# Second expert table: token-major products instead of feature-major, and no closing transposes

## The reference, cut to what matters

```python
def chunk(args):
    x_c, e_c, g_c = args
    u = u_tab[e_c]
    vv = v_tab[e_c]
    a = jax.nn.gelu(jnp.einsum('cd,chkd->chk', x_c, u).astype(jnp.float32), approximate=False)
    return jnp.einsum('chk,chkd->cd', (g_c * a).astype(vv.dtype), vv)
...
x = x + gate2[:, None, :] * peer_ffn(h2, ...)
return rmsnorm(x, norm_final_g)
```

## Time and profile before

| | |
|---|---|
| median of 3 runs | 1925.5 us (1924.06 to 1925.86) |
| span of the profiled execution | 1923.2 us |
| what lies around the span, by these runs | 0.9 to 2.7 us, 2.3 at the median |
| TensorE busy / VectorE busy / ScalarE busy | 91% / 67% / 47% |
| bytes from memory, mean rate | 280 MB, 147 GB/s |
| half A / half B | 1478 to 1719 us / 1721 to 1906 us |

### The profile page before, as it was taken

One profiled execution on the slowest core, in us unless ns is written; L12 is line 12 of the kernel. 1 busy time (PEld: TensorE's weight loads), 2 busy tenths in 40 slices (PEclk: granted clock), 3 DMA queues, 4 the chain that ended last, 5 costly groups with the idle time before them and its releaser, 6 DMA issues.

```text
span 1923.2 us, 32571 instructions
## 1 busy us (share of the span) xinstructions
PE 1748.6 (91%) x11846; PEld 1612.2 (84%) x11846; DVE 1286.6 (67%) x2392; ACT 906.5 (47%) x1411; POOL 23.9 (1%) x50
## 2 busy tenths in 40 slices
PE   6788898898978886997979999999999999999996
PEld 5677777796767675886779999899999999999996
DVE  3666557544755686444656999777777888875554
ACT  4474355344534573443335666555554333334443
POOL 0000000000000000000000000000000000000000
PEclk8898897898979997995989999999999999999999
DMA  6423443344325435450443444443343434355552
GB/s 224 172 102 104 162 165 110 132 174 155 110 88 187 148 132 190 145 195 22 151 143 145 175 175 174 153 145 139 132 150 123 141 133 151 131 177 186 183 177 85
DMA packets 40324, 282.97 MB, mean 147 GB/s; under 512 B 5280, under 2 KB 5424, under 8 KB 6848
## 3 DMA queue, kind: packets, MB, share of 16 engines
q1 hardware_dynamic: 37136, 267.13, 39.3%
q0 software_dynamic: 3120, 14.94, 2.2%
HBM read 279.94 MB, written 2.12 MB: 147 GB/s over the span
## 4 chain that ended last, share of the span: by engine, by line
PE 73%; DVE 17%; ACT 4%; DMA 3%; issue 3%; DVEq 0%; SPq 0%; ACTq 0%
PE banks L504 20%; PE banks L506 19%; PE banks L505 19%; PE banks L771 6%; DVE w_lo L1065 5%; DMA raw<-stream 3%; PE banks L577 2%; PE banks L546 2%; PE banks L591 1%; ACT w_hi L834 1%; PE banks L603 1%; PE banks L602 1%; PE banks L601 1%; DVE arena L1447 1%; DVE arena L1254 1%
## 5 line engine op out<-in xcount | busy, mean ns | idle before, releaser
L1065 DVE TENSOR_TENSOR w_lo<-raw,w_hi 128x1024 fp32r<-128x1024 f32 x504 | 614.3, 1221 | 393.5 <-ACT w_hi L834 391.5
L834 ACT ACTIVATE w_hi<-raw 128x1024 fp32r<-128x1024 f32 x504 | 532.0, 1056 | 652.1 <-PE banks L506 557.3
L504 PE MATMUL banks<-xT_hi,w_hi 128*128 128x256 f32 x2384 | 689.1, 289 | 7.6 <-DVE w_lo L1065 2.9
L506 PE MATMUL banks<-xT_hi,w_lo 128*128 128x256 f32 x2384 | 678.3, 285 | 0.0
L505 PE MATMUL banks<-xT_lo,w_hi 128*128 128x256 f32 x2384 | 677.9, 284 | 0.0
L504 PEld LDWEIGHTS banks<-xT_hi,w_hi 128*128 128x128 f32 x2384 | 461.5, 194 | 9.6 <-ACT arena L993 2.9
L505 PEld LDWEIGHTS banks<-xT_lo,w_hi 128*128 128x128 f32 x2384 | 460.7, 193 | 0.0
L506 PEld LDWEIGHTS banks<-xT_hi,w_lo 128*128 128x128 f32 x2384 | 460.1, 193 | 0.0
L504 PE MATMUL banks<-w_hi,xT_hi 128*128 128x512 f32 (+2 forms) x628 | 249.4, 397 | 24.4 <-DVE xT_lo L1097 15.9
L505 PE MATMUL banks<-w_lo,xT_hi 128*128 128x512 f32 (+2 forms) x628 | 246.5, 393 | 0.0
L506 PE MATMUL banks<-w_hi,xT_lo 128*128 128x512 f32 (+2 forms) x628 | 246.2, 392 | 0.0
(11 more groups left out here) (182 smaller groups left out, 1593.1 us busy)
## 6 DMA issues: line engine op xcount, KB each, us to landing
raw<-stream SPq DMA_DIRECT2D x252, 1024.0 KB, 4.8
arena<-ln_in POOLq DMA_DIRECT2D x4, 1024.0 KB, 4.9
arena<-mod_rows POOLq DMA_DIRECT2D x1, 3072.0 KB, 9.4
arena<-g_in POOLq DMA_DIRECT2D x3, 512.0 KB, 10.4
arena<-x_in SPq DMA_DIRECT2D x1, 1024.0 KB, 5.1
arena<-bands_in POOLq DMA_DIRECT2D x1, 1024.0 KB, 5.1
arena<-keys_in POOLq DMA_DIRECT2D x1, 1024.0 KB, 5.1
x_spill<-arena POOLq DMA_DIRECT2D x1, 1024.0 KB, 5.0
```

Source lines behind the costliest of these rows:

```text
L504: pe.matmul(out, stationary[0], moving[0], start=first, stop=False, **k)
L506: return pe.matmul(out, stationary[1], moving[0], start=False, stop=last, **k)
L834: act.activation(w_hi[:, s], raw[:, s // 2, (s % 2) * PIECE:(s % 2 + 1) * PIECE], ACT.Copy).then_inc(piece_hi, 1)
L1065: dve.tensor_tensor(w_lo[:, s], raw[:, s // 2, (s % 2) * PIECE:(s % 2 + 1) * PIECE], w_hi[:, s].bitcast(F32), ALU.subtract).then_inc(piece ...
```

## The change

`second_table` gets the operands exchanged: for each half `b` of the tokens the 128 experts x 128 tokens of `xT_hi`, `xT_lo` are stationary, and 512 columns of the piece move, twice. That is 2 x 2 x 3 = 12 matmuls of 512 columns. Bank `2 b + d` then holds tokens by features. `backT`, its two copies, the 16 transposes and two semaphores are gone; VectorE's closing reads banks 0 to 3 at once.

```diff
--- before.py
+++ after.py
@@ -259,7 +259,7 @@
         hot1 = scratch[:, 0:512].rearrange("p (k t n) -> p k t n", k=2, t=GT)
         hot2 = scratch[:, 512:1536].rearrange("p (k t n) -> p k t n", k=2, t=GT)
 
-        backT, x_end, gate2, final_gain, y_end = cut(0, KD, S), cut(2048, B, D), cut(4096, D), cut(5120, D), cut(6144, B, D)
+        x_end, gate2, final_gain, y_end = cut(2048, B, D), cut(4096, D), cut(5120, D), cut(6144, B, D)
         hidden = arena[:, :].rearrange("p (n t) -> p n t", t=S)
 
 
@@ -376,7 +376,7 @@
         wf_split = sem("wf_split")
         key_matched = sem("key_matched")
         hot_ready, g_full, g_taken = sem("hot_ready"), sem("g_full"), sem("g_taken")
-        back_copied, back_full, rms_ready, stored = sem("back_copied"), sem("back_full"), sem("rms_ready"), sem("stored")
+        rms_ready, stored = sem("rms_ready"), sem("stored")
 
         evac_sem = {"act": evac_act, "dve": evac_dve}
 
@@ -776,10 +776,11 @@
 
                 pe.wait_ge(piece_lo, FIRST_V + j + s + 1)
                 pe.wait_ge(hidden_lo, j + s + 1)
-                for d in range(KD):
-                    mm = parts_product(banks[:, d // 2, (d % 2) * S:(d % 2 + 1) * S],
-                                       [x[:, s, d * P:(d + 1) * P] for x in (w_hi, w_lo)], [xT_hi[:, s], xT_lo[:, s]],
-                                       False, False, skip_group_check=True)
+                for b in range(B):
+                    for d in range(D // COLS):
+                        mm = parts_product(banks[:, 2 * b + d], [x[:, s, b * P:(b + 1) * P] for x in (xT_hi, xT_lo)],
+                                           [x[:, s, d * COLS:(d + 1) * COLS] for x in (w_hi, w_lo)],
+                                           False, False, skip_group_check=True)
                 mm.then_inc(piece_used, 1)
 
             wait_put(pe, E["scores"])
@@ -809,12 +810,6 @@
             with pe.Fori(0, HALF // RING) as i:
                 for s in range(RING):
                     second_table(RING * i + HALF, s)
-            pe.wait_ge(back_copied, 2)
-            for b in range(B):
-                for d in range(KD):
-                    mm = pe.transpose(banks[:, 4 + 2 * b + d // 4, (d % 4) * P:(d % 4 + 1) * P],
-                                      backT[:, d, b * P:(b + 1) * P], ident)
-                mm.then_inc(back_full, 1)
 
         @block.scalar
         def _(act):
@@ -1034,8 +1029,6 @@
             with act.Fori(0, HALF // RING - 1) as i:
                 for s in range(RING):
                     refill(RING * i + HALF, s, True, True)
-            act.wait_ge(piece_used, n_pieces)
-            act.activation(backT[:, 0:4], banks[:, 0:2].rearrange("p q (a t) -> p (q a) t", a=2), ACT.Copy).then_inc(back_copied, 1)
             act.wait_ge(x_ready, DEPTH + 2)
             for b in range(B):
                 link(act.activation(y_end[:, b], x_end[:, b], ACT.Square, accum_out=small[:, 8 + b:9 + b]))
@@ -1544,11 +1537,9 @@
                     rest_of_piece(FIRST_V + HALF + RING * i + RING, s)
                     rest_of_hidden(RING * i + HALF + RING, s)
             dve.wait_ge(piece_used, n_pieces)
-            dve.tensor_copy(backT[:, 4:8], banks[:, 2:4].rearrange("p q (a t) -> p (q a) t", a=2)).then_inc(back_copied, 1)
             dve.wait_ge(end_loaded, 48)
             for b in range(B):
-                dve.wait_ge(back_full, b + 1)
-                flat = banks[:, 4 + 2 * b:6 + 2 * b].rearrange("p q n -> p (q n)")
+                flat = banks[:, 2 * b:2 * b + 2].rearrange("p q n -> p (q n)")
                 link(dve.tensor_tensor(y_end[:, b], flat, gate2, ALU.mult))
                 link(dve.tensor_tensor(x_end[:, b], x_end[:, b], y_end[:, b], ALU.add))
             dve.sem_inc(x_ready, 1)
```

## The result

The changed kernel takes 1907.4 us (median of 4 runs, 1906.2 to 1908.8) against 1925.7 us before (4 runs); the ratio is 0.9901, 95% interval [0.9887, 0.9915]. That is 18.3 us faster. 22.2 us and 1903.3 us were forecast, and the forecast's upper end was 1907.0. The profiled execution has a span of 1906.3 us, 16.9 less than before.

What follows compares the result with a forecast made beforehand. TensorE was taken to bound the kernel; half B 10.3, half A 9.4 and the closing 2.5 us sum to 22.2 us, taking the median from 1925.5 to 1903.3 us, range 1901.0 to 1907.0.

Steps and rivals of the forecast that it cites:

- What bounds the kernel: TensorE, busy 91% of the span and 73% of the chain that ended last, sets the pace in both halves.
- the 0.0134 us a matmul has beside its columns: Fixed cost of each TensorE matmul whatever its length; twelve of these go per piece in both halves.
- Half B, 10.3 us: Half B's 64 pieces: 2.720 us each instead of 2.881, 0.161 saved per piece, 10.3 us in all.
- the slower rival: Late chunks in half B make TensorE wait and its clock fall; 1941.7 us with 16 pieces slow, chance 0.03.
- Half A, 9.4 us: Half A's 64 pieces: twelve matmuls take 2.734 us between gates, 0.147 saved per piece, 9.4 us in all.
- low end of 5.8: Half A's smallest gain, 5.8 us, if its blocks of twelve take 0.2325 us a matmul throughout.
- The closing, 2.5 us: At the end, VectorE's first product starts where its copy did, 1905.78 instead of 1908.27: 2.5 us saved.
- The cover: Other engines and transfers keep up: VectorE still waits 0.2 us a piece in half A; half B's chunks every 5.44 us.
- Neither VectorE nor the stream became the bound: Two rivals: VectorE bounds half A, 1912.7 us, chance 0.05; the stream of transfers bounds half B, 1913.6 us, chance 0.04.
- only the columns count: Rival: the extra 0.0134 us belongs to the projections' place, so only the closing gains; 1923.0 us, chance 0.05.
- The range: 1901.0 to 1907.0 us: both ends of half A's cost, the lower end reduced by 1.4 us for the fastest run; rivals excluded.
- The sign that everything before half A would stand to within a microsecond: In the profile after, all before half A, zero matmuls included, should stand as it did to within a microsecond.

Runs made afterwards that it cites:

- e4: The changed kernel run again unaltered, beside the single edits, against the kernel before: 1907.9 us (4 runs), ratio 0.9908.
- e2: The kernel before with the new product form in half A alone; half B, copies and transposes as before: 1921.5 us (8 runs), ratio 0.9975.
- e9: The changed kernel unaltered once more, its third profiled execution, for the clock at half B's start: single run 1908.5 us.
- e6: The changed kernel without the gates' matmuls beside half A, semaphores still counted up: 1885.8 us (one run).
- e3: The kernel before with the new product form in half B alone; half A, copies and transposes as before: 1917.3 us (6 runs), ratio 0.9954.
- e5: The changed kernel with half A doing two pieces, then two groups' gates (blocks of 24 matmuls): 1907.9 us (5 runs), ratio 0.9902 to the kernel before.

## Why the forecast came out 4 us too fast

By the medians some 4 us of the forecast gain did not come, by the traces 5.3: 3.0 in half A, 1.6 in half B, and 0.6 because half A began that much later, which is scatter from one execution to the next.

- *What bounds the kernel, and the 0.0134 us a matmul has beside its columns:* right. Half B's 0.2268 us a step in e4 is the projections' pace. The Trainium skill (TensorE: Matmul & The Clock Gate, Back-to-back issue gap) gives 2.5 ns beside the columns, as the gap of an isolated matmul; here a step in a long stream, 0.2267 us less 512 columns at 2.4 GHz, leaves 13.4 ns. By its figure the gain would have been about 6 us, as an estimate, and 18 were measured.
- *Half B, 10.3 us:* right where the clock holds. The missing term is the clock. I saw it fall behind a wait of 16 us, took the slower rival's only trigger to be late chunks, and did not ask the same of the 2 us between the halves, a wait of 1.98 us for `xT_lo` that stood in rows 4 and had not cost anything in the one execution of before. It costs 1.6 us in some executions, and 1.5 with the old form (e2).
- *Half A, 9.4 us:* the mechanism held, and this is the term that was sized wrong. I had two rows, 0.2267 from the fifth matmul on the earlier trace rows and 0.2325 for blocks of six, and followed the first because its operands were the same. Blocks between other work were the better likeness: 0.231 on the average, so that the whole block was slow and not its first four steps, and 6.4 us, near the low end of 5.8 that the second row gave.
- *The closing, 2.5 us:* right, in the changed kernel and alone.
- *The cover:* VectorE's wait in half A was forecast at 0.2 us and is 0.27; TensorE waited for no transfer. Neither VectorE nor the stream became the bound, and e4's 0.2268 us a step rules out that only the columns count. The slower rival did not come as it was priced, but the sign that was to tell of it, a granted clock under 1.00, did: the clock fell for another reason than late chunks.
- *The range:* its upper end carried half A's low bound but no scatter above the median and no clock; the measured 1907.4 lies 0.4 us above it. The sign that everything before half A would stand to within a microsecond does not hold either: in e9 half A starts 2.3 us later than before.

## What to carry to other kernels

With the same columns in total, fewer and longer matmuls save a fixed cost each (13.4 ns here), but only a stream that runs on long enough gets the full pace: take the price from a row whose block is as long as yours and stands between the same kind of work, before one with the same operands. Choosing which operand moves can also choose the layout of the sum, and save a transpose at the end. A wait of two microseconds on TensorE's path is worth looking at for what follows it: here the clock fell behind it in six of ten executions, and a single profile, like the one of before, can miss it.

## What the hardware showed unexpectedly

- Matmuls of 512 columns in this kernel take 0.231 us a step for the first six to eleven steps of a block and 0.2267 after that. It is there behind small matmuls (the changed kernel), behind a wait of 0.39 us (e6), behind a wait of 1.98 us in e9 and not in e4, and once more after the clock has risen again (six steps of 0.233 us from 1720.07 in the changed kernel). The old form of 256 columns shows nothing like it: 0.12 from the second step on.
- In the changed kernel TensorE's pace fell to the 1.2 GHz level 1.2 us after it had resumed from a 2 us wait, and stayed there for eight steps; in half B alone (e3) it came after 0.5 us. In e5 the clock was already down when TensorE resumed, and thirteen steps were slow.
- From one profiled execution of the changed kernel to the next, half A starts anywhere between 1477.1 and 1480.1 us. From there to the end of the span it is 426.3 us where the clock held and 427.8 where it fell. So in these four executions the larger part of the scatter lies ahead of the part that was changed.
